# Attention projections on one Trainium2 core: the mean squares of queries and keys in four column strips, spread through DRAM

## What is computed

```python
def rms_norm(x, gain):
    xf = x.astype(jnp.float32)
    xf = xf * lax.rsqrt(jnp.mean(xf * xf, axis=-1, keepdims=True) + RMS_EPS)
    return (xf * gain.astype(jnp.float32)).astype(x.dtype)
...
    k = rms_norm(k.reshape(bsz, t, B_HEADS, B_DH), k_norm)
...
    q = rms_norm(q.reshape(bsz, t, B_HEADS, B_DH), q_norm)
    o = forgetting_attention(q, k_all, v_all, c_all)
    o = o.reshape(bsz, t, B_WIDTH).astype(x.dtype) * jax.nn.silu(gate)
    return x + o @ w_o
```

## Time and profile before

| | us |
|---|---|
| runs | 1521.09, 1524.19, 1525.02 |
| median | 1524.19 |
| the profiled execution | 1523.4 |
| its span | 1521.7 |
| TensorE busy | 1483.1 (97%) |
| VectorE busy | 996.8 (66%) |
| ScalarE busy | 685.7 (45%) |
| GpSimd busy | 414.0 (27%) |

### The profile page before, as it was taken

How to read it: one execution, slowest core, us unless ns; L and a number is a source line. 1 busy time by engine, 2 the same in 40 slices (tenths; PEclk the granted TensorE clock), 3 DMA queues, 4 the chain that set the end, 5 groups by cost and what they waited for, 6 DMA issues and landing times.

```text
span 1521.7 us, 23184 instructions
## 1 busy us (share of the span) xinstructions
PE 1483.1 (97%) x8353; PEld 1093.3 (72%) x8353; DVE 996.8 (66%) x1987; ACT 685.7 (45%) x1380; POOL 414.0 (27%) x335
## 2 busy tenths in 40 slices
PE   6999999999999999999999999999999999989998
PEld 6888888888888885445777777777677777764443
DVE  6868696878778684126467676768677677757421
ACT  4445555544445453212265555645555555545100
POOL 5012322121212201012051534343442525332200
PEclk9999999999999999999999999999999999999999
DMA  9682928466473933423236869595977779598731
GB/s 270 187 241 80 295 72 260 127 194 189 139 229 99 288 114 115 113 81 128 61 115 189 265 190 314 181 284 183 283 236 229 264 218 307 175 332 318 244 137 57
DMA packets 289411, 296.81 MB, mean 195 GB/s; under 512 B 25722, under 2 KB 247098, under 8 KB 289298
## 3 DMA queue, kind: packets, MB, share of 16 engines
q1 hardware_dynamic: 278162, 258.75, 56.0%
q0 software_dynamic: 11136, 36.59, 6.6%
HBM read 239.90 MB, written 122.50 MB: 238 GB/s over the span
## 4 chain that ended last, share of the span: by engine, by line
PE 81%; ACT 6%; DMA 6%; DVE 5%; issue 1%; SPq 1%; POOL 0%; DVEq 0%; POOLq 0%; ACTq 0%
PE psum L2117 39%; PE psum L2141 7%; PE psum L2624 7%; PE psum L2424 4%; PE psum L2450 4%; PE psum L2194 3%; DMA arena<-block_rows 2%; PE psum L2080 2%; PE psum L2384 2%; DMA block_rows<-arena 2%; PE psum L2482 2%; ACT psum L1257 2%; ACT psum L1266 1%; DVE arena L1802 1%; PE psum L2205 1%
## 5 line engine op out<-in xcount | busy, mean ns | idle before, releaser
L2117 PE MATMUL psum<-arena 128*128 128x252 f32 (+1 forms) x3472 | 811.9, 384 | 2.8 <-DVE arena L1434 2.7
L2117 PEld LDWEIGHTS psum<-arena 128*128 128x128 f32 x3472 | 641.3, 190 | 124.2 <-issue 24.4
L940 POOL TENSOR_TENSOR arena<-arena 128x1024 f32<-128x1024 f32 x64 | 152.0, 2375 | 373.2 <-DMA arena<-k_pages 365.8
L1434 DVE TENSOR_TENSOR arena<-arena,psum 128x252 f32<-128x252 f32 (+1 forms) x310 | 129.6, 418 | 175.1 <-PE psum L2117 168.3
L2624 PE MATMUL psum<-arena 128*128 128x512 f32 x256 | 115.9, 605 | 4.2 <-DMA arena<-o_heads 2.6
L1015 ACT COPY arena<-psum 128x252 f32<-128x252 f32 (+1 forms) x124 | 46.4, 374 | 156.7 <-PE psum L2117 156.6
L2141 PE MATMUL psum<-arena 128*128 128x512 f32 x256 | 113.0, 594 | 0.1
L2624 PEld LDWEIGHTS psum<-arena 128*128 128x128 f32 x256 | 47.7, 192 | 62.4 <-issue 60.0
L2141 PEld LDWEIGHTS psum<-arena 128*128 128x128 f32 x256 | 47.5, 190 | 57.4 <-issue 56.5
L1068 ACT ACTIVATE arena<-arena 128x1024 f32<-128x1024 f32 x48 | 50.6, 1055 | 78.3 <-DVE arena L1478 78.2
L1257 ACT ACTIVATE psum<-psum,arena 128x640 f32<-128x640 f32 (+3 forms) x64 | 58.9, 921 | 59.0 <-DVE arena L1781 59.0
(11 more groups left out here) (267 smaller groups left out, 2108.5 us busy)
## 6 DMA issues: line engine op xcount, KB each, us to landing
k_pages<-in_cache_k SPq DMA_DIRECT2D x64, 512.0 KB, 6.6
v_pages<-in_cache_v SPq DMA_DIRECT2D x64, 512.0 KB, 7.2
arena<-k_pages SPq DMA_DIRECT2D x64, 512.0 KB, 5.2
arena<-v_pages SPq DMA_DIRECT2D x64, 512.0 KB, 6.9
arena<-in_w_in_a SPq DMA_DIRECT2D x32, 512.0 KB, 6.8
arena<-in_x_prompt SPq DMA_DIRECT2D x16, 512.0 KB, 8.1
arena<-in_w_kv SPq DMA_DIRECT2D x16, 512.0 KB, 6.7
arena<-in_w_in_b SPq DMA_DIRECT2D x16, 512.0 KB, 8.2
```

Of the source, the lines that this page charges most:

```text
L940: pool.tensor_tensor(k_ring[:, m % 2], k_ring[:, m % 2], q_all[:, m % S:m % S + 1, :].broadcast_to([P, PAGES, P]), ALU.mult).then_inc(kq_m ...
L1434: dve.tensor_tensor(out, more, bank[n % 2][:, 0:size(u)], ALU.add).then_inc(of.by_dve, 1)
L2117: ins = pe.matmul(bank[n % 2][:, 0:size(u)], w[:, k, :], x[:, k, :], start=(k == 0 and r in (0, 1, 3, 4)), stop=(k == HK - 1), skip_group_ ...
```

## The change

The mean of one token is the same number on 64 partitions. After the change PE does not write it 64 times: it uses 32 columns of `bones` (48 to 79: 16 of head 0 and 16 of head 1), and puts four products of 258 columns into four groups of 32 partitions of one bank. ACT needs one logarithm and one exponential of 128 x 258 for each side, in place in `sq[y]`. SP stores one partition of each head and strip into a DRAM scratch (two transfers, `rs_out`) and loads the rows back, each spread over the 64 partitions of its head (two transfers, `rs_in`). `norm` on DVE waits for both. `sq[0]` and `sq[1]` become two halves of one area.

```diff
     def means(q):
-        return [(f"m{y}{i}", q) for y in "kq" for i in range(3)]
+        return [("mk", q), ("mq", q)]
...
+            def rs_out(q):
+                sp.wait_ge(strips_set, 2 * (q + 1))
+                if q:
+                    sp.wait_ge(rs_done, 32 * q)
+                for x in range(2):
+                    src = sq_both[16 * x:P:32].rearrange("p (y n) -> p y n", y=2)[:, :, 0:W4]
+                    sp.dma_start(rs_rows[x].rearrange("y (s n) -> s y n", n=W4), src).then_inc(strips_stored, 16)
+
+            def rs_in(q):
+                sp.wait_ge(strips_stored, 32 * (q + 1))
+                for x, rows in enumerate(HEAD):
+                    sp.dma_start(sq_both[rows], rs_rows[x].rearrange("y n -> (y n)").partition_broadcast(DH)).then_inc(rs_done, 16)
+
+            rs_out(0)
+            rs_in(0)
             sp.wait_ge(b_units.done, kq_b(0, 14))
...
                 load_row(p, 5)
+                rs_out(p + 1)
+                k_in(m + 4)
+                rs_in(p + 1)
                 if p:
                     v_in(p, 0, 0, 1)
-                k_in(m + 4)
                 store_row(p, 6)
                 load_row(p, 6)
+                k_in(m + 5)
                 sp.wait_ge(b_units.done, kq_b(p + 1, 14))
...
-                k_in(m + 5)
                 store_row(p, 7)
...
+            def rs_strips(q, y):
+
+                n = items.at("m" + "kq"[y], q)
+                act.wait_ge(items.done, n)
+                act.activation(sq[y][:, 0:W4], bank[7][:, 0:W4], ACT.Ln, bias=eps).then_inc(items.taken, 1)
+                act.wait_ge(items.taken, n)
+                act.activation(sq[y][:, 0:W4], sq[y][:, 0:W4], ACT.Exp, scale=-0.5).then_inc(strips_set, 1)
...
             def norm(q, y):
 
-                dve.wait_ge(rs_done, 2 * q + y + 1)
+                dve.wait_ge(rs_done, 32 * (q + 1))
...
-            def means(q, y, *ns):
-                for n in ns:
-                    dst = open_item(f"m{'kq'[y]}{n}", q)
-                    pe.wait_ge(sq_done, 2 * q + y + 1)
-                    pe.matmul(dst[:, 0:W3], bones, sq[y][:, part3(n)], start=True, stop=True, skip_group_check=True).then_inc(items.done, 1)
+            def means(q, y):
+                dst = open_item("m" + "kq"[y], q)
+                pe.wait_ge(sq_done, 2 * q + y + 1)
+                for n in range(4):
+                    ins = pe.matmul(dst[32 * n:32 * n + 32, 0:W4], bones[:, DH - 16:DH + 16], sq[y][:, n * W4:(n + 1) * W4],
+                                    start=True, stop=True, skip_group_check=True)
+                ins.then_inc(items.done, 1)
...
                 scores(p, 2)
+                kq_n(0)
                 if p:
                     weighted(p - 1, 3)
-                kq_n(0)
-                turn_values(p, 0)
-                if p:
-                    decode(p - 1, 0)
                 kq_n(1)
                 last((0, 0, 3))
+                turn_values(p, 0)
+                if p:
+                    decode(p - 1, 0)
                 turn_rows(p, 2)
-                if p:
-                    turn_num(p - 1, 0)
                 turn_values(p, 1)
                 kq_n(2)
+                if p:
+                    turn_num(p - 1, 0)
```

More of the change, by code:

```diff
@@ L152 @@
 W3 = N // 3
+W4 = N // 4
 AH = 8
@@ L1911, in _ @@
             vg_add(0, 3)
-            norm(0, 0)
             vg_add(0, 4)
@@ L1915, in _ @@
             vg_add(0, 6)
+            norm(0, 0)
             dve.wait_ge(raw_set, 1)
@@ L1940, in _ @@
                     score(m - 4)
-                    score(m - 3)
                 vg_add(p, 10)
@@ L1949, in _ @@
                 vg_add(p, 12)
+                if p:
+                    score(m - 3)
                 vg_add(p, 13)
@@ L2518, in pair @@
                 scores(p, 2)
+                kq_n(0)
                 if p:
                     weighted(p - 1, 3)
-                kq_n(0)
+                kq_n(1)
+                last((0, 0, 3))
                 turn_values(p, 0)
```

72 lines of the change are left out of this document (20 added, 52 removed).

## The result

The changed kernel takes 1557.88 us (median of 4 runs, 1556.64 to 1562.28) against 1522.64 us for the kernel before on the same chip: ratio 1.0225, 95% interval 1.0206 to 1.0245. It is 35 us slower. The forecast was 1517, within 1501 to 1531: wrong in sign and outside its range. The profiled span is 1557.0 us.

What follows compares the result with a forecast made beforehand. TensorE, busy 97% of the span, was taken as the bound. Gains of 2.0 us before the first pair, 1.5 in pair 0 and 3.0 over six rounds made 6.5: 1523.4 to 1517 us, 8 in 10 within 1501 to 1531.

Steps and rivals of the forecast that it cites:

- Strips on PE: Mean blocks on PE: four column strips run side by side, 0.53 us a block, relieving PE of 2.8 us a pair.
- Strips in a row: Rival, mean blocks on PE: strips do not overlap, 1.74 us a block, 1528 us; chance 0.03.
- Strips set at t = 3.8, in DRAM at 6.9, the chain of 6.5 us on DVE: Round from first mean: strips ready at 3.8, stored by 6.9; DVE needs 6.5 us from spread landing to PE's unit 7.
- I take 6.0: the spread lands at t = 13.0 (11.6 to 13.85): Load back from DRAM: 1.06 MB takes 6.0 us, so unit 7 starts at 19.5, keeping 1.5 of 3.4 us.
- A spread of 7 us or longer: Sign of being wrong, on the load back from DRAM: would point to no change or slower by the queue.
- The queue wins back 2.8 us of idle time: Transfer queue: 2.8 of about 4.7 us idle absorb the spread's 4.0; row 7's reload lands at about 40.3, round gains 0.5.
- slower by the queue: Rival: slow spread, queue wins back only 1.4 us, row 7's reload 3.45 us late, 1531 us; chance 0.20.
- no change: Rival: spread transfer takes 4.85 us at the 32-partition store rate, lands at 13.85, 1522.5 us; chance 0.28.
- nothing is blocked twice: Moved decode product, its transpose and DVE's sum: same order behind the next unit on both engines, so no added blocking.
- nothing there is urgent: Sample score moved behind three DVE additions: k page freed some 5 us later, delaying SP's next loads without harm.
- Before the first pair, "2.0": Start, before pair 0: PE saves 2.4 us, the spread ends 0.4 us too late for DVE, leaving 2.0 us gained.
- All of it hidden: Rival: spread as fast as a 128-partition load, taken in the queue's idle time; gain 26 us, 1497 us; chance 0.12.

Runs made afterwards that it cites:

- filler: Changed kernel with 14 extra matmuls of 128x252, result written over, between units 5 and 6 in each of seven rounds; 1563.19 us, ratio 1.0258.
- filler_short: Changed kernel with 8 extra matmuls, result written over, between units 5 and 6 in each of seven rounds; 1553.39 us, ratio 1.0185.
- norm_late: Changed kernel with DVE's two normalisations of the next pair moved behind the unit-5 and unit-6 additions, DRAM spread kept; 1546.63 us, ratio 1.0147.
- mended: norm_late with the two value loads behind the reload of row block 6 and the sixth page load back behind the weight loads; 1554.89 us, ratio 1.0189.
- shifts_only: Kernel before with only the moved sample steps and the moved page load, no DRAM scratch; 1531.56 us, ratio 1.0047.
- no_spread: Changed kernel without the DRAM store and load back, so queries and keys are scaled by wrong values; 1519.75 us, ratio 0.9962.
- no_spread_page: no_spread with the sixth page load put back behind the next pair's weight loads; 1514.02 us, ratio 0.994.
- late_no_spread: norm_late without the DRAM spread, so queries and keys are scaled by wrong values; 1519.38 us, ratio 0.9967.

## Why the prediction was wrong, step by step

- **Strips on PE: right, the margin too small.** Blocks of 0.58 us against 0.53. The first unit behind each is up to 0.2 us longer than before (1.89 for 1.69), which is the cost of going in and out of the form that I had put at 0.1 in the sum, and at 0.1 for either side in the sentence on the drain; it is of the kind that the Trainium skill names ("TensorEngine Tiling (Array Packing)", section "Key Properties"), and smaller than the 0.3 at either side that I had priced as the rule. Counted from start to start, the mean blocks fell from 30.7 to 9.2 us, 21.5 less. "Strips in a row" is out.
- **Strips set at t = 3.8, in DRAM at 6.9, the chain of 6.5 us on DVE: right**, 4.1, 7.1 and 6.3 (916.47 to 922.79).
- **"I take 6.0: the spread lands at t = 13.0 (11.6 to 13.85)": the step that failed first.** It landed at 17.3 in the round shown, 3.4 beyond my high bound. I took the duration from two loads of 512 KB over 128 partitions with no other load ahead of them on the queue and moved it into a stretch whose share is 0.88. Even with empty queues it was 7.4; in the rounds 7.9 to 10.7. The bound from above was a rate, and it held no wait behind other transfers, not even the k page that the change itself issues between the strips' store and the spread. By my own sum 17.3 + 6.5 = 23.8 for unit 7 against 21.0 before: a loss of 2.8 us a round where I had a gain of 1.5. A spread of 7 us or longer stood among my signs of being wrong, but the rivals that it pointed to ended at 1522.5 and 1531, or 1539 with nothing won back: none of them held this wait.
- **What idle time costs beyond itself: missing.** PE's clock had been at 1.00 in the rounds, and no step asked what an idle time of 2.4 to 4.6 us does to it. It put 14.9 us on the units, and filler took them off again; of the run time filler_short got back 4.5.
- **"The queue wins back 2.8 us of idle time", reload at t = 40.3: the mechanism was right, its size not, and it was hidden.** In the changed kernel the reload cost 0.9 us, since PE had been held up before by the same load. With that wait out of the way it cost 15.8 (norm_late) to 25.9 us (mended), and in norm_late the reload landed at t = 41.1 to 43.2 in six rounds, not at 40.3. This is the rival "slower by the queue", which had 0.20 and 1531, t = 42.55; norm_late, at 1546.6, comes nearest to that rival by itself, with the transposes of row 7 waiting for row 6's store as a second place I had not seen. The 4.7 us of idle time behind the 2.8 do not follow from the row either: a share of 0.88 leaves 3.9 of 32.5 us; 4.7 come out only if stretches of 2 us with shares above 1 count as 1. With 3.9 the same sum ends near the rival "no change". There, 41.15 - 1.69 - 39.1 is 0.36 and not 0.3, so its time is 1522.9.
- **The moved sample steps, "nothing is blocked twice", "nothing there is urgent": wrong by some 7 us** (shifts_only). Two places are shown. Without the DRAM step the moved page load starts GpSimd's multiplication at t = 23.6 instead of 26.3, onto DVE's new product (3 to 6 us between no_spread and no_spread_page); I had followed what the load delays and not what it starts. In shifts_only that product was never hit; there the moved weighted sum saved 3.8 us of reload waits and the turns of row 3 gave 5.6 back, behind DVE's small output steps and row_max 3. Why that is more than was saved is not settled.
- **Before the first pair, "2.0": mis-sized.** From the first mean to the first scores PE took 16.55 us instead of 17.43, a gain of 0.9; the scores waited 1.2 us for the normalisation, where I had 0.4.
- **"All of it hidden", 26 us, would have been wrong too with a free load:** no_spread gains 5 us and no_spread_page 9. Of the 21 us that PE saves, most went to waits that had just been covered: the turns of row blocks 0 and 3 for ScalarE (7.3 to 12.4 us instead of 3.1), and unit 4 for ScalarE's copy (0.41 us in seven rounds).

The balance of the two profiled spans, +35.3 us: idle time of the units +27.3, of the turns +7.2, of the last projection and the scores +4.5, of the reload -4.2, busy time +1.6, small groups the rest. In the busy time, counted from start to start, the mean blocks' -21.5 stand against +19.4 for the units, of which +5.7 stay in no_spread, which has no idle time over 0.6 us in front of a unit. The units behind the strips make up 2.4 of these; the rest is not explained.

## What to carry to other kernels

Here 1.06 MB a round, in a stretch where the transfer engines had a share of 0.88 before the change, cost 27 us, although almost nothing waited for the load itself. Price such a transfer by the time that the transfer engines need in that stretch, add what is issued just ahead of it, and look which reload is next, before you look at who reads it. In a kernel that is balanced to within a microsecond, a wait removed shows the next one; so test each suspected wait in a version in which the others are gone (norm_late against late_no_spread), or it will look free. When a load moves, ask what its landing starts, not only what it delays.

## What the runs showed of the hardware

- A DVE product of two SBUF operands, 165 ns by itself, stood for 2.3 us until a GpSimd product of 128x1024 that ran beside it was done. The row maxima, which read PSUM and one SBUF operand, kept their 0.3 us beside GpSimd's work in the kernel before (1003.02, GpSimd from 1002.76 on). The Trainium skill ("SBUF — State Buffer", section "Who interferes with whom") has this as a lock on a port pair that the two engines share, held for a whole instruction; the trace agrees, to within 0.03 us at its end.
- After each idle time of 2.4 to 4.6 us ahead of unit 7 the granted clock was at half (0.5) for some microseconds, about 34 us over the seven rounds more than in the kernel before. With 14 matmuls in each idle time it was 1.00 between 700 and 1420 us, with 8 of them 0.99, in the changed kernel 0.97.
- A row of 8256 bytes read from DRAM to 64 partitions, twice, took 7.4 us in an empty queue for 1.06 MB, slower than the 6.0 of 1 MB to 128 partitions; as one transfer to 128 partitions it took 6.4.
